# RWKV-7 layer: the carried state scaled and added on VectorE instead of through identity products on TensorE

## The reference, cut to what matters

```python
def step(s, inp):
    w_t, k_t, v_t, kk_t, a_t = inp[:5]
    sa = jnp.einsum('bhvk,bhk->bhv', s, kk_t)
    s = (s * w_t[:, :, None, :]
         - sa[..., None] * (kk_t * a_t)[:, :, None, :]
         + v_t[..., None] * k_t[:, :, None, :])
    y = jnp.einsum('bhvk,bhk->bhv', s, inp[5]) if len(inp) > 5 else None
    return s, y
```

## Time and profile before

| | |
|---|---|
| median of 3 runs | 5268.63 us |
| the profiled execution, its own time | 5257.98 us |
| its span, first to last instruction | 5256.2 us |
| granted TensorE clock, mean over the span | 0.966 |
| busy share of the span: TensorE, VectorE, ScalarE, GpSimd | 90%, 50%, 35%, 25% |
| steps of the recurrence, first and last `carry` | 3575.8 and 4970.2 us |

### The profile page before, as it was taken

One profiled execution on the slowest core, in us unless ns is written; L12 is line 12 of the kernel. 1 busy time (PEld: TensorE's weight loads), 2 busy tenths in 40 slices (PEclk: granted clock), 3 DMA queues, 4 the chain that ended last, 5 costly groups with the idle time before them and its releaser, 6 DMA issues. The chain is left out here.

```text
span 5256.2 us, 121695 instructions
## 1 busy us (share of the span) xinstructions
PE 4710.6 (90%) x49854; PEld 2635.2 (50%) x49854; DVE 2605.3 (50%) x4105; ACT 1816.4 (35%) x4359; POOL 1297.3 (25%) x2820
## 2 busy tenths in 40 slices
PE   6999997999999998999999999967878888888689
PEld 3666663333333333454444444436666666666544
DVE  2444444667666661231222222245666666666476
ACT  1221212433434330231212111135556656555322
POOL 0111111222222220000000000005555565565333
PEclk8999997999999998999999999988999999999899
DMA  5222221000000007331111211135666666666485
GB/s 203 93 85 89 86 75 53 23 23 11 17 23 22 24 21 287 139 136 51 60 60 65 67 60 60 56 93 137 148 151 141 152 145 147 150 152 149 111 271 169
DMA packets 925174, 526.39 MB, mean 100 GB/s; under 512 B 658581, under 2 KB 876309, under 8 KB 916632
## 3 DMA queue, kind: packets, MB, share of 16 engines
q1 hardware_dynamic: 843482, 496.91, 32.8%
q10 hardware_dynamic: 81216, 22.73, 2.1%
HBM read 331.00 MB, written 188.49 MB: 99 GB/s over the span
## 5 line engine op out<-in xcount | busy, mean ns | idle before, releaser
L1611 PE MATMUL p_bU<-keep_hT,p_slab 128*128 128x512 f32 (+1 forms) x2592 | 1029.9, 559 | 12.5 <-DMA p_slab<-in_o_w_in_dram 7.0
L1611 PEld LDWEIGHTS p_bU<-keep_hT,p_slab 128*128 128x128 f32 x2592 | 493.6, 191 | 543.7 <-issue 512.3
L924 PE MATMUL at_bS<-at_qT,at_kT 97*64 97x512 f32 (+1 forms) x2368 | 611.3, 602 | 4.0 <-ACT at_pT L1022 2.3
L1059 DVE TENSOR_REDUCE at_mx<-at_bM 128x1 f32<-128x512 f32 (+1 forms) x656 | 391.0, 627 | 268.6 <-PE at_bM L889 265.2
L1022 ACT ACTIVATE at_pT<-at_bS 128x512 f32<-128x512 f32 (+1 forms) x592 | 339.9, 591 | 429.8 <-PE at_bS L924 360.4
L1683 DVE SCALAR_TENSOR_TENSOR p_z<-p_u,p_shift,p_z 128x2306 f32<-128x2306 f32 x26 | 68.2, 2621 | 770.2 <-ACT p_z L1641 770.2
L1938 POOL TENSOR_TENSOR rw_g_at<-rw_g_at,rw_g_prod 64x14 f32<-64x14 f32 (+6 forms) x1008 | 314.4, 312 | 79.0
L1936 POOL TENSOR_TENSOR rw_g_prod<-rw_g_at 64x14 f32<-64x14 f32 (+6 forms) x1008 | 311.8, 309 | 79.1
L1080 DVE TENSOR_TENSOR at_sum_vector<-at_sum_vector,at_pT 128x512 f32<-128x512 f32 x320 | 300.8, 940 | 43.6 <-ACT at_pT L1022 28.2
L2395 DVE TENSOR_TENSOR rw_S<-rw_bank,rw_dec 128x128 f32<-128x128 f32 x288 | 84.1, 292 | 452.2 <-PE rw_bank L2116 452.2
L943 PE MATMUL at_bO<-at_pT,at_va 128*64 128x512 f32 x1152 | 301.9, 602 | 0.0
(11 more groups left out here) (270 smaller groups left out, 9499.8 us busy)
## 6 DMA issues: line engine op xcount, KB each, us to landing
rw_zin<-scratch_heads SPq DMA_DIRECT2D x144, 512.0 KB
rw_XB<-scratch_inverses SPq DMA_DIRECT2D x576, 64.0 KB
scratch_heads<-p_z SPq DMA_DIRECT2D x24, 1024.0 KB, 4.9
rw_lin<-scratch_lora SPq DMA_DIRECT2D x144, 128.0 KB
scratch_bv<-rw_bv SPq DMA_DIRECT2D x144, 128.0 KB
scratch_products<-rw_NB SPq DMA_DIRECT2D x288, 64.0 KB
scratch_y<-rw_ysb ACTq DMA_DIRECT2D x288, 64.0 KB, 2.7
p_slab<-in_o_w_in_dram SPq DMA_DIRECT2D x34, 512.0 KB, 5.8
```

The source lines that it names most:

```text
L924: last = pe.matmul(bS[rows, g % 3, 0:nq * P], kT[:, s, k * P + VH * x:k * P + VH * x + VH], qT[:, s, q0 * P:(q0 + nq) * P], start=True, st ...
L1059: nc.vector.tensor_reduce(mx[:, j, piece:piece + 1], bM[:, (FIRST_ITEM[b] + i) % 2, 0:n], AX.X, ALU.max).then_inc(max_red, 1)
L1611: last = pe.matmul(bU[:, n % 4, 0:w], slab[:, i, k, :], hT[:, k, tok:tok + w], start=(k == 0), stop=(k == KD - 1))
```

## The change

`step_begin` no longer adds the old state to `SU` through the identity. VectorE keeps a second tile, `S_decayed`, made directly behind each `carry` by one multiplication of `S` with the next chunk's decay. `carry` becomes two `scalar_tensor_tensor` instructions, one per direction, that compute `SU * decay + S_decayed`.

```diff
-        S = core.sb("S", [P, 2, C])
+        S, Sd = core.sb("S", [P, 2, C]), core.sb("S_decayed", [P, 2, C])
+        sd_done = sem("rw_state_decayed")
...
                         for rows, other in ACROSS:
-                            pe.matmul(SU[rows, C * d:C * d + C], ident[rows, rows], S[rows, d, :],
-                                      start=False, stop=False, skip_group_check=True)
                             pe.matmul(Y[other, C * d:C * d + C], AR[rows, n.six, d, u, 1, :], S[rows, d, :],
...
-                def carry(n, c):
+                def decayed_state(n, c):
 
                     if c == 0:
                         v.wait_ge(dec_part, 2 * n.n + 2)
                         if n.group == NG - 1:
                             v.wait_ge(dec_last, n.pair + 1)
+                    v.wait_ge(s_out, 4 * n.n + c)
+                    nc.vector.tensor_tensor(Sd[:], S[:], dec[:, n.kept, :, c, None].broadcast_to([P, 2, C]), ALU.mult).then_inc(sd_done, 1)
+
+                def carry(n, c):
+
                     v.wait_ge(su_mm, 4 * n.n + c + 1)
-                    nc.vector.tensor_tensor(S[:], SU[:, 0:2 * C].rearrange("p (d v) -> p d v", d=2),
-                                            dec[:, n.kept, :, c, None].broadcast_to([P, 2, C]), ALU.mult).then_inc(s_out, 1)
+                    v.wait_ge(sd_done, 4 * n.n + c + 1)
+                    if 4 * n.n + c == 0:
+                        v.wait_ge(dec_part, 2)
+                    for d in range(2):
+                        last = nc.vector.scalar_tensor_tensor(out=S[:, d, :], in0=SU[:, C * d:C * d + C], scalar=dec[:, n.kept, d, c:c + 1],
+                                                              in1=Sd[:, d, :], op0=ALU.mult, op1=ALU.add)
+                    last.then_inc(s_out, 1)
+                    if c < NCH - 1:
+                        decayed_state(n, c + 1)
+                    elif n.n + 1 < NBODY:
+                        decayed_state(n.on(1), 0)
...
+                nc.vector.memset(Sd[:], 0.0).then_inc(sd_done, 1)
```

## The result

The changed kernel takes 5289.31 us, the median of 5 runs (5278.07 to 5299.83), beside 5268.26 us for the kernel before (5265.32 to 5269.36). The ratio is 1.0042, with a 95% interval of 1.0025 to 1.0059: 22 us slower, from 13 to 31. The profiled execution took 5289.31 us, 31 more than that of before.

A forecast was written before the change was run, and what follows sets the result against it. No engine is full, so a chain bounds it: two meet at L2116, VectorE's through `XT` and ScalarE's queue. +18 (copy), +1 (last bodies), -2 (quarters), -8 (issue) give +9 us, 5278 as median; range 5247 to 5304.

The forecast's parts named there:

- three outcomes: Whole kernel: slower 0.46, within 0.2% 0.34, faster by over 0.2% 0.20.
- TensorE's term: Four identity products a step leave TensorE: -2 us for time on the quarters, -8 us for issue stalls.
- slower carry; copies of steps 1 to 3: VectorE: `S` comes 0.20 us later but is covered except in the last bodies, +1 us; these copies have cover.
- copy in front of `XT`, lateness: VectorE behind carry 3: everything to `XT` 0.5 us late, 0.25 a body at L2116, +18 us (+12 to +30).
- copy in front of `XT`, clock: TensorE in step 0: not in the sum; a rival had `low_rank` at 1.2 GHz in a third of bodies, +26 us.
- the least distance from `low_rank` to L2116: TensorE in step 0: 0.99 us from the start of `low_rank` to L2116 taken as about the least.
- the size of the wait for `XT`: TensorE before `step_sa` of step 0: grows from 1.08 us to about 1.5 a time.
- worth nothing: TensorE in step 0: arriving 0.22 us earlier gains nothing, as ScalarE's queue and VectorE are waited for.
- All three signs of being wrong: First step not 0.2 to 0.3 us longer; stretch's granted clock below 0.97; "issue" moving by more than 20 us.
- slower by a second mechanism: TensorE in step 0: idle from about 1.7 us lowers the clock, +26 us on top of 9, 5304; chance 0.17.
- TensorE bound: TensorE is the limit: quarters' time counts in part and stalls thin by 20 us, -23, 5246; chance 0.20.
- the issue term: TensorE's "issue" stalls: 6% fewer packets, gain 8 us (0 to 20), idle from 87 to about 79 us.

The follow-up runs named there:

- tensor half: Kernel before without the identity products, carry left as it was, old state's own term missing: 0.9952 of the kernel before, 5243.72 us.
- vector half: Kernel before with identity products kept, carry pair adding a tile of zeros, decayed copy made but not read: 1.0068 of the kernel before, 5304.25 us.
- vector half, copy moved: The vector half with the decayed copy for step 0 made behind the `XT` additions: 1.0008 of the kernel before.
- filler: Changed kernel plus eight unused 128-column products a body on TensorE in the wait for `XT`: 1.0002 of the kernel before, 5268.40 us.
- copy moved: Changed kernel with the decayed copy for step 0 behind the `XT` additions instead of behind carry 3: 0.9976 of the kernel before, 5255.96 us.

## Why the prediction was right, and where it was not

Slower was the likeliest of the three outcomes in the prediction, and the time is 11 us above the one given, inside the range. That the total came so close is in part luck: the clock added some 21 us that the sum did not have, and TensorE's term gave 12 more than it had. By its own terms:

| term | forecast | measured |
|---|---|---|
| quarters and instructions, removed from TensorE | -10 | -22 (tensor half) |
| slower carry; copies of steps 1 to 3 | +1 | +4, not told from 0 (vector half, copy moved) |
| copy in front of `XT`, lateness | +18 | about 14 (what the filler leaves of 35); 19 (bodies at the full clock) |
| copy in front of `XT`, clock | 0, a rival of 26 | about 21 (filler) |
| sum | +9 | +17, by the filler; the change itself +22 (13 to 31) |

**The mechanism** was the forecast's: the copy behind carry 3 is the only one without cover, everything to `XT` comes 0.58 us later in most bodies (0.52 forecast), and the carry pair takes 0.48 us (0.49 forecast). Hardly anybody waits for `S` in the others: L2083 waited 0.7 us in 4 times in the stretch of 3600 to 4900, and 5.3 us in 17 times over the whole program, nearly all of it in the last bodies, for which the forecast had 1 us; 5 was the mark. ScalarE's `Vt` copies still started when its queue was free. That an earlier `XT` is worth nothing and a later one costs was shown by moving `bonus` in both kernels. The price of the lateness, 0.25 us a body, was right at the full clock: 0.27 there. One step of its working was not. The prediction took 0.99 us for about the least distance from `low_rank` to L2116; over bodies 4 to 66 the least is 0.86 and the lower quartile 0.89. With 0.99 its 0.5 us late would give 0.37 on the mean, with 0.86 it gives 0.27.

**The failed step** is the size of the wait for `XT` and what hung on it. "TensorE's wait for `XT` grows from 1.08 us to about 1.5" took only the later end: the 0.22 us by which TensorE arrives earlier, "worth nothing" in the forecast, are true waiting time as well. I also put 0.5 where 0.58 came. The trace has 1.92. The wait alone was worth nothing either way in the sum, but its length decides on the clock. Over the kernels, waits of 1.29 us (tensor half) and 1.40 (copy moved) went with 5 and 1 falls in a step 0 of 63 bodies, 1.72 (vector half) with 20, 1.92 with 35. All three signs of being wrong that I had set came. The clock was 0.94, below 0.97. The first step, carry 3 to carry 0, grew by 0.62 us (6.31 to 6.93), not by 0.2 to 0.3; in the bodies at the full clock it grew by 0.26. And the idle for "issue" fell from 86.7 to 65.5 us, by 21, where 79 was forecast and 20 was the mark; as the tensor half alone has 80.9, the rest of that fall came with VectorE's part, and why is open. The rival "slower by a second mechanism" deserved more than 0.17: its point of decision, "about 1.7 us", stood in the prediction, and my sum for the wait left out a term of the same forecast. Against it I held bodies whose two waits of step 0 add up to 1.9 us at the full clock; but those are two waits with work between them, and they say little on one wait of 1.9. Nor did they all hold: the one step 0 of the trace before in which the clock fell had waits of 1.18 and 0.93 us, while two with 2.2 and 2.4 together kept it.

**The TensorE term** was half of what it is. The rival "TensorE bound" had 33 us of gain there, 13 of them time on the quarters and 20 of stalls. That the gain is larger than 10 was right and was hidden by the clock, but not the reasons: one column instead of 64 gained nothing, and the stalls gave 6. For the idle of "issue" the tensor half shows 80.9 us against the forecast of 79, so that by itself this part was right and the other -16 us lie elsewhere, in what no idle time shows. The Trainium skill (Runtime: NRT & Kernel Launch, Instruction fetch mechanics) has fetching hidden, by which the issue term would be 0. This case's traces differ: the stalls behind the packets are there, 86.7 us in all, and went to 80.9 with fewer instructions and to 99.0 with more. Whether the rest of the 22 and 36 us is fetching, no run shows.

**Open** are: what in a product of one column costs time; why +6% costs 36 us and -6% gives 22; the exact split between lateness and clock; and whether the longer waits for the masks cost anything. The carry alone, without the copies, was not run.

## What to carry to other kernels

When a change takes work off the engine that waits and puts it on the engine that it waits for, add both to the wait, and then look at what the granted clock did behind waits of the new length in the trace that you have. An instruction that nobody needs soon goes behind the one that another engine waits for: the same copy cost 32 to 35 us in front of `XT`, and behind it nothing that can be measured. A product with few columns is not a cheap product: count the products before their columns.

## What the runs showed of the hardware

- A mean wait of 1.72 us (vector half) or 1.92 (changed kernel) before `step_sa` went with a fall of TensorE's clock from 2.4 to 1.2 GHz in 20 and 35 of 63 steps 0. In the kernels with a mean wait of 0.5 to 1.4 us it was 0 to 5; where it was 0.5 us, in the kernel before with `bonus` moved, the 5 followed other waits of 1.50 to 1.92 us. The lower clock came after the wait, with TensorE fully busy again (granted 0.50 in the window from 3657.20).
- Work of no use in that wait made the kernel 21 us faster than it was without.
- Four one-column products more in a step, a record of which takes 181 ns against 225 for 64 columns, cost 36 us over 288 steps, 0.12 us a step. One column instead of 64 in the products that are there changed nothing (1.0001).
- All 41 "issue" stalls of TensorE over 1 us in the trace before end 1.25 to 1.69 us after a 16 KiB packet of the instruction queue has landed.
- `scalar_tensor_tensor` with a scalar from a tile, on 64 columns from PSUM, takes 0.280 us and a pair of them 0.48; the instruction that reads what the pair wrote starts 0.03 to 0.10 us after its end.
